# A five-layer network in fp32 pairs on one core: copies ahead of casts, a second raw chunk, and moved lows and splits

## The chip, the cores and the metric

The kernel runs on one core of one Trainium2 chip. The metric is the device time of the whole launch in microseconds (us), the median of several runs. The engines are TensorE (PE), VectorE (DVE), ScalarE (ACT), GpSimd (POOL) and SyncE (SP), which here issues most transfers.

## What is computed

x has 256 tokens and 1024 features. Four layers and a fifth one follow each other; cut to what matters:

```python
for layer in range(4):
    h = rmsnorm(x, attn_norm[layer])
    m = (diff_attention, stick_breaking_attention, sliding_window_attention)[layer % 3](h, ...)
    x = x + m @ w_o[layer]
    h = rmsnorm(x, ffn_norm[layer])
    x = x + (silu(conv(h @ w_gate)) * conv(h @ w_val)) @ w_down[layer]     # 2752 wide, 3 taps
x = rmsnorm(x, final_norm)
h = rms_norm(x, g_mix_pre)                                                 # the fifth layer
u, q, k, v = split(h @ w_in)
y = concatenate([pool_mixer(u), moba_attention(q, k, v)]) @ w_out          # pooled and attention halves
x = x + rms_norm(y, g_mix_post)
h = rms_norm(x, g_ffn_pre)
x = x + rms_norm((gelu(conv(h @ w_gate)) * (h @ w_val)) @ w_down, g_ffn_post)
x = x + (p @ w_ple) * sigmoid(x @ w_ple_gate)
```

Layers 0 and 3 use differential attention, layer 1 stick-breaking, layer 2 the sliding window. All is fp32.

## The kernel before

**Number pairs.** Every fp32 matrix is split in a high part (a cast to fp32r) and a low part (what is left). A product is three matmuls (high x high, high x low, low x high; L1681 to L1683, with the moving part 256 tokens). A weight chunk is 128 x 2048 numbers, which is two tiles of 128 output features over 8 tiles of 128 inputs: 48 matmuls. SP loads chunk after chunk into three raw buffers; ACT casts each to w_hi (L394); DVE subtracts to w_lo (L919, `split_to`), which signals lo_ready; w_hi and w_lo have five slots. SP loads chunk c once DVE has made the low of chunk c - 3.

**Stages.** STAGES lists da, sb, sw or mix (the projections and the attention of a layer; "mix" is the fifth, with pooled features), wo, up (22 chunks), down (8), and at the end gate. Each engine has one program, written out by hand in the same order of stages, and waits on semaphores for the others. `ahead(c, lead)` and `split_to(c)` put casts or lows of coming weight chunks at chosen places between other work. Results of a chunk go to one of three PSUM banks (pj, and val_bank in the up stage); bank_free gives a bank back.

**Normalisation.** To begin a stage before the root mean square is known, the first chunks are multiplied with the raw x times its gain (`raw_high` L448 on ACT, `raw_low` on DVE or POOL); DVE scales the result by rstd (`scaled_first` L985, or L1444 in the up stage). `raw_chunks` says where the normalised h takes over: `normalise` makes hf on DVE (L965), `split_h` casts it on ACT (L444), and the lows are made by DVE for even tiles (L961) and by POOL for odd ones (`low_odd`, L1544). PE puts the matmul that sums the squares (`statistic`, L1842) between tiles of the first raw chunk, at the place that one line gives:

```python
elif raw not in (None, "x", "raw") and k == {"d": 2, "w": 4}.get(raw[0], 5):
```

h_hi is written anew only when PE has used the raw tile (raw_used).

**Up stage.** Per chunk DVE has four taps of the convolution on top of ACT's first term (L1454, L854), then a w_lo, then the product (L1471); POOL casts the product and makes its low (L1652, L1655). In the first two chunks (one in the fifth layer) the taps read scaled copies in u_sb, not the banks.

**Attention.** In the sliding layer eight steps j each have on PE: transposes of the probabilities, scores for step j + 2, some projection or output products, and the head matmuls (L1916, L1917), which want ACT's copies of the transposed probabilities (`copy_probT`, L472) and, since all steps share one bank, DVE's low of the last step's result (`mix_low`, L1072, behind ACT's `mix_high`, L478). DVE reads the scores (L1001, `take`), makes a w_lo, divides by the sum (L1033 to L1040) and makes that low. In the stick-breaking layer POOL masks the probabilities (L1626) before the heads.

**Fifth layer.** `add_normed` (L1058, L1067) adds the normalised result of wo and of the last down stage to x; tmp holds a copy that ACT made of the PSUM bank (L785, L881).

## Time and profile before

| what | value |
|---|---|
| median of 3 runs | 1498.96 us (1498.57 to 1501.03) |
| profiled execution | 1498.88 us, its span 1497.2 us |
| PE busy | 1487.0 us, 99% of the span |
| DVE, ACT, POOL busy | 1063.5 (71%), 879.2 (59%), 336.2 us (22%) |
| matmuls | 11576 |
| transfers | 265.16 MB, mean 177 GB/s |

The span runs from the first to the last instruction of the program; the time of an execution also has what lies around it. Stages of the profile that the text speaks of: the first layer begins at 0, its up stage at some 124 us; the stick-breaking layer's attention ends at some 418, the sliding layer's attention runs from 614 to 694; the fifth layer begins at 1178.8, its up stage at 1263, its last down stage ends at 1464. A busy matmul row also counts the time in which it overlaps the next one, so starts tell more than durations; idle time stands in brackets behind a row, with the instruction whose semaphore ended it.

### The profile page before, as it was taken

The numbers are of one execution on the slowest core, as the hardware profiler recorded it, in microseconds if no ns is written. First come the engines' busy times: TensorE is split into PE (matmuls) and PEld (weight loads), VectorE is DVE, ScalarE is ACT, GpSimd is POOL, SyncE is SP. The second block draws the span as 40 slices with busy tenths as digits, with TensorE's granted clock in tenths as the row PEclk, the third lists the DMA queues.
The fourth block names the chain that finished last, engine by engine and source line by source line (L and its number), as shares of the span: only waits on it lengthen the run. The fifth ranks groups of instructions, "written<-read, shape, count | busy, mean of one in ns | idle before, by whom it ended". The sixth has DMA issues, their size and how long they took to land.

```text
span 1497.2 us, 28533 instructions
## 1 busy us (share of the span) xinstructions
PE 1487.0 (99%) x11576; PEld 1423.4 (95%) x11576; DVE 1063.5 (71%) x1734; ACT 879.2 (59%) x1405; POOL 336.2 (22%) x482
## 2 busy tenths in 40 slices
PE   9999999999999999999999999999999999999998
PEld 8999999899999998989999899999998899999998
DVE  7778877565578775786887566688775778776545
ACT  7777655456766554575656347766563567544343
POOL 2103222211142222213222221032222371221101
PEclk9999999999999999999999999999999999999999
DMA  7643656443336554552665545446554554365450
GB/s 272 204 162 124 242 184 218 169 163 147 117 138 218 205 190 177 187 180 85 216 207 183 188 170 178 155 145 221 197 192 177 173 191 169 114 228 194 164 209 29
DMA packets 39694, 265.16 MB, mean 177 GB/s; under 512 B 5247, under 2 KB 5562, under 8 KB 8976
## 3 DMA queue, kind: packets, MB, share of 16 engines
q1 hardware_dynamic: 36432, 255.54, 48.4%
q0 software_dynamic: 2992, 7.79, 2.3%
q8 instruction: 91, 1.49, 0.4%
q14 instruction: 35, 0.29, 0.1%
q10 hardware_dynamic: 144, 0.05, 0.0%
HBM read 262.24 MB, written 1.12 MB: 176 GB/s over the span
## 4 chain that ended last, share of the span: by engine, by line
PE 87%; DVE 8%; ACT 3%; issue 1%; POOL 0%; ACTq 0%
PE bank L1681 21%; PE bank L1682 20%; PE bank L1683 20%; PE bank L1692 9%; PE bank L1691 4%; PE bank L1733 4%; DVE w_lo L919 4%; PE bank L1742 2%; ACT w_hi L394 1%; PE bank L1916 1%; DVE tmp L1454 1%; PE bank L1897 1%; PE bank L1896 1%; DVE tmp L965 1%; PE bank L1905 1%
## 5 line engine op out<-in xcount | busy, mean ns | idle before, releaser
L919 DVE TENSOR_TENSOR w_lo<-w_raw,w_hi 128x2048 fp32r<-128x2048 f32 x239 | 553.0, 2321 | 72.5 <-ACT w_hi L394 72.3
L1681 PE MATMUL bank<-h_hi,w_hi 128*128 128x256 f32 x1968 | 561.2, 285 | 0.8 <-DVE w_lo L919 0.8
L1682 PE MATMUL bank<-h_lo,w_hi 128*128 128x256 f32 x1968 | 556.8, 283 | 0.0
L1683 PE MATMUL bank<-h_hi,w_lo 128*128 128x256 f32 x1968 | 556.8, 283 | 0.0
L394 ACT CAST w_hi<-w_raw 128x2048 fp32r<-128x2048 f32 x239 | 453.0, 1905 | 85.3 <-DMA w_raw<-w_std 64.4
L1681 PEld LDWEIGHTS bank<-h_hi,w_hi 128*128 128x128 f32 x1968 | 377.3, 192 | 6.4 <-issue 4.2
L1682 PEld LDWEIGHTS bank<-h_lo,w_hi 128*128 128x128 f32 x1968 | 377.4, 192 | 0.1
L1683 PEld LDWEIGHTS bank<-h_hi,w_lo 128*128 128x128 f32 x1968 | 377.3, 192 | 0.0
L1692 PE MATMUL bank<-act_both,w_hi 128*128 128x512 f32 x672 | 239.0, 399 | 0.0
L1454 DVE SCALAR_TENSOR_TENSOR tmp<-bank,par,tmp 128x255 f32<-128x255 f32 (+1 forms) x346 | 149.1, 476 | 94.6 <-ACT tmp L854 93.5
L1691 PE MATMUL bank<-act_both,w_lo 128*128 128x256 f32 x672 | 188.9, 281 | 0.0
L854 ACT ACTIVATE tmp<-bank,par 128x256 f32<-128x256 f32 x173 | 88.8, 558 | 157.0 <-PE bank L1683 156.9
L1692 PEld LDWEIGHTS bank<-act_both,w_hi 128*128 128x128 f32 x672 | 126.4, 188 | 30.0
L1652 POOL CAST act_both<-tmp 128x256 f32 x110 | 53.7, 488 | 440.2 <-DVE tmp L1471 336.5
L1681 PE MATMUL bank<-act_both,w_hi 128*128 128x256 f32 x516 | 149.2, 289 | 0.0
L1682 PE MATMUL bank<-act_both,w_hi 128*128 128x256 f32 x516 | 145.9, 283 | 0.0
L1683 PE MATMUL bank<-act_both,w_lo 128*128 128x256 f32 x516 | 145.9, 283 | 0.0
L1691 PEld LDWEIGHTS bank<-act_both,w_lo 128*128 128x128 f32 x672 | 127.0, 189 | 0.0
L1733 PE MATMUL bank<-h_hi,w_hi 128*128 128x256 f32 x384 | 102.5, 289 | 0.0
L1681 PEld LDWEIGHTS bank<-act_both,w_hi 128*128 128x128 f32 x516 | 98.7, 191 | 3.0 <-issue 2.7
L1733 PE MATMUL bank<-h_hi,w_lo 128*128 128x256 f32 x384 | 100.3, 283 | 0.0
L1682 PEld LDWEIGHTS bank<-act_both,w_hi 128*128 128x128 f32 x516 | 98.8, 191 | 0.1
(219 smaller groups left out, 2116.2 us busy)
## 6 DMA issues: line engine op xcount, KB each, us to landing
w_raw<-w_std SPq DMA_DIRECT2D x239, 1024.0 KB, 4.8
act_both<-vec_dram POOLq DMA_DIRECT2D x56, 128.0 KB, 3.4
w_raw<-w_std SPq DMA_DIRECT2D x3, 512.0 KB, 7.8
x<-xT SPq DMA_DIRECT2D x2, 512.0 KB, 5.2
out<-x SPq DMA_DIRECT2D x3, 256.0 KB, 2.0
w_raw<-w_std SPq DMA_DIRECT2D x2, 256.0 KB, 4.8
par<-params SPq DMA_DIRECT2D x1, 446.0 KB, 6.0
cst<-consts SPq DMA_DIRECT2D x1, 256.0 KB, 8.8
```

Source lines behind the costliest of these rows:

```text
L394: act.copy(w_hi[:, n % SLOTS, :], w_raw[:, n % RAW, :]).then_inc(hi_ready, 1)
L854: act.activation(to[:, slot, :], source, ACT.Identity, bias=col(3), scale=col(2)).then_inc(conv_init, 1)
L919: dve.tensor_tensor(w_lo[:, n % SLOTS, :], w_raw[:, n % RAW, :], w_hi[:, n % SLOTS, :].bitcast(F32), ALU.subtract).then_inc(lo_ready, 1)
L1454: return dve.scalar_tensor_tensor(to[:, slot, lag:S], source(v)[:, 0:S - lag], par[:, bass.ds(at + (4 * v + 2 - lag), 1)], to[:, slot, lag:S],
L1652: pool.tensor_copy(act_hi[:, bass.ds(j, 1), :].squeeze(1) if not isinstance(j, int) else act_hi[rows, j, :], cval[rows, slot, :]).then_inc ...
L1681: pe.matmul(dst, wh, xh, start=first, stop=False, skip_group_check=shared)
L1682: pe.matmul(dst, wh, xl, start=False, stop=False, skip_group_check=shared)
L1683: done = pe.matmul(dst, wl, xh, start=False, stop=last, skip_group_check=shared)
L1691: pe.matmul(bank[:, 0:S], wl, xh, start=start and k == 0, stop=False, skip_group_check=True)
L1692: done = pe.matmul(bank[:, :], wh, pair, start=False, stop=stop and k == len(weights) - 1, skip_group_check=True)
L1733: pe.matmul(dst, a, b, start=k == 0 and w is wh and (n == 0 or not shared), stop=False, skip_group_check=shared)
L1742: done = pe.matmul(dst, a, b, start=False, stop=k == DT - 1, skip_group_check=shared)
```

## The change

1. **Sliding layer.** On ACT the copies of the probabilities for steps 2 and 6 go ahead of a weight cast or of the exponentials, `mix_high` ahead of `evac_q`, and in step 5 ahead of the copies of step 6 and of the exponentials. On DVE `mix_low` goes ahead of `divide`.
2. **Stick-breaking layer, last group.** DVE's first `mix_low` goes between the two w_lo.
3. **First layer.** ACT's cast and DVE's low of weight chunk 2 go ahead of the rstd.
4. **Up stages of layers 0 to 3.** In the second chunk, as in the first, DVE's w_lo goes ahead of the taps; PE's fifth chunk waits for the scaled tiles of the second and no longer for its bank.
5. **Fifth layer, start.** The second chunk is multiplied with the raw x too; DVE scales its result, which ACT copied before; the statistic is asked for behind tile 5 instead of tile 2.
6. **Last up stage.** DVE makes all eight lows of h, each one tile behind the normalised tile (`every=True`); POOL's `low_odd` is left out there.
7. **Gains.** ACT multiplies by mix_post and ffn_post when it copies the banks to tmp (two instructions of 256 for one of 512 in wo), and `add_normed` on DVE is a product of two tensors instead of three factors.

```diff
@@ -292,3 +292,3 @@
 
-            return 3 if app == 0 else 2 if app % 2 and app < 9 else 1
+            return 3 if app == 0 else 2 if app % 2 and app < 9 or app == 8 else 1
 
...
@@ -567,2 +567,4 @@
                     groups = 2 if kind == "mix" else 4
+                    if c0 == 0:
+                        split_to(2)
                     (both_rms if prev == "down3" else rms)(SUMS[prev][2])
...
@@ -581,8 +583,4 @@
                         for k in range(2):
-                            if k:
-                                act.wait_ge(bank_free, RING + c0 + 1)
-                                act.wait_ge(used, c0 + k + 1)
-                                act.copy(u_sb[:, 2 * k:2 * k + 2, :].rearrange("p a b -> p (a b)"),
-                                         pj[slot_of(c0, k)][:, :]).then_inc(bank_free, 1)
                             ahead(c0 + k)
+                        act.wait_ge(bank_free, RING + c0 + 2)
                         lead = 2
...
@@ -745,10 +743,16 @@
                             q, s = half + j, s_half + j
-                            copy_probT(s, j % 2, 2)
+                            if j not in (2, 6):
+                                copy_probT(s, j % 2, 2)
                             if j == 5:
                                 ahead(c0 + 6, HIGH)
+                                mix_high(q, j)
+                                copy_probT(s + 1, 0, 2)
                             if j < 6:
                                 exps(s + 2, j % 2, j + 3)
+                            if j != 5:
+                                mix_high(q, j)
                             if j in (1, 3):
                                 evac_q(c0 + 4 + j // 2, j // 2)
-                            mix_high(q, j)
+                            if j == 1:
+                                copy_probT(s + 1, 0, 2)
                             if j < 3:
...
@@ -784,3 +788,4 @@
                                     mixed_gains[:, t:t + 1]).then_inc(mixed_high, 1)
-                        done = act.copy(tmp[:, a:b, :].rearrange("p a b -> p (a b)"), source)
+                        for t in range(a, b):
+                            done = act.mul(tmp[:, t, :], source[:, (t - a) * S:(t - a + 1) * S], param("mix_post", t))
                         if k != 3:
...
@@ -880,3 +885,4 @@
                             squares(name, k, pj[slot_of(c0, k)][:, 0:S])
-                            act.copy(tmp[:, k, :], pj[slot_of(c0, k)][:, 0:S]).then_inc(bank_free, 1)
+                            act.mul(tmp[:, k, :], pj[slot_of(c0, k)][:, 0:S], param("ffn_post", k))\
+                               .then_inc(bank_free, 1)
                             if k == 2:
...
@@ -954,3 +960,3 @@
 
-            def normalise(app, norm, behind=None):
+            def normalise(app, norm, behind=None, every=False):
 
...
@@ -961,3 +967,3 @@
                     dve.tensor_tensor(h_lo[:, k, :], hf[:, k, :], h_hi[:, k, :].bitcast(F32),
-                                      ALU.subtract).then_inc(h_lo_even, 1)
+                                      ALU.subtract).then_inc(h_lo_odd if k % 2 else h_lo_even, 1)
 
...
@@ -966,4 +972,10 @@
                                              ALU.mult, ALU.mult).then_inc(hf_done, 1)
-                    if k % 2 and k > 1 and behind is None:
+                    if every:
+                        if k:
+                            low(k - 1)
+                    elif k % 2 and k > 1 and behind is None:
                         low(k - 3)
+                if every:
+                    low(DT - 1)
+                    return
                 if behind is not None:
...
@@ -1054,7 +1066,6 @@
 
-            def add_normed(gain, factor, signal, after):
+            def add_normed(factor, signal, after):
 
                 def scaled(k):
-                    dve.scalar_tensor_tensor(tmp[:, k, :], tmp[:, k, :], param(gain, k),
-                                             factor, ALU.mult, ALU.mult).then_inc(dve_step, 1)
+                    dve.tensor_tensor(tmp[:, k, :], tmp[:, k, :], factor, ALU.mult).then_inc(dve_step, 1)
                     steps[0] += 1
...
@@ -1141,5 +1152,5 @@
 
+                split_to(2)
                 dve.wait_ge(rstd_done, 1)
                 scaled(0, 1, 2, 3)
-                split_to(2)
                 scaled_first(0, proj, (0.125, 1.0))
...
@@ -1202,2 +1213,4 @@
                                      {"mix": (1.0, 1.0), "sw": (0.125, 0.125)}.get(kind, (0.125, 1.0)))
+                        if kind == "mix":
+                            scaled_first(c0 + 1, u_sb[:, 2:4, :], (1.0, 1.0))
                     app += 1
...
@@ -1312,4 +1325,5 @@
                                 ahead(c0 + n)
-                                ahead(c0 + n, HIGH)
                             mix_low(q, i * 2)
+                            if not more:
+                                ahead(c0 + n, HIGH)
                             mix_low(q + 1, i * 2 + 1)
...
@@ -1339,5 +1353,5 @@
                                 ahead(c0 + 3 + min(j, 4))
+                            mix_low(half + j, j)
                             if j < 6:
                                 steps[0] += divide(s_half + j + 2, j % 2, True, steps[0])
-                            mix_low(half + j, j)
                         half += 8
...
@@ -1395,5 +1409,5 @@
                         dve.wait_ge(rstd_done, SUMS[name][2] + 1)
-                        add_normed("mix_post", mix_rstd, x_ready, sum_behind)
+                        add_normed(mix_rstd, x_ready, sum_behind)
                         ahead(c0 + 2, AHEAD)
-                        normalise(app, SUMS["res_a"][2])
+                        normalise(app, SUMS["res_a"][2], every=True)
                         ahead(c0 + 1, AHEAD)
...
@@ -1445,4 +1459,3 @@
                                                       ALU.mult).then_inc(first_scaled, 1)
-                                if j == 0:
-                                    split_to(weights_of(layer, c) + RING)
+                                split_to(weights_of(layer, c) + RING)
 
...
@@ -1639,3 +1652,4 @@
                     raw_low(app)
-                    low_odd(app, hf)
+                    if layer < 4:
+                        low_odd(app, hf)
                     app += 1
...
@@ -1750,3 +1764,3 @@
                             statistic("x")
-                    elif raw not in (None, "x", "raw") and k == {"d": 2, "w": 4}.get(raw[0], 5):
+                    elif raw not in (None, "x", "raw") and k == (5 if raw == "down3" else {"d": 2, "w": 4}.get(raw[0], 5)):
                         statistic(raw)
...
@@ -1768,6 +1782,6 @@
 
-            def project(c, slot, app=None, raw=None):
+            def project(c, slot, app=None, raw=None, release=True):
 
                 if app is not None:
-                    pair(c, (pj[slot][:, 0:S], pj[slot][:, S:2 * S]), app, raw=raw)
+                    pair(c, (pj[slot][:, 0:S], pj[slot][:, S:2 * S]), app, raw=raw, release=release)
                     return
...
@@ -1949,5 +1963,6 @@
                     g0 = c0 + lead
-                    for k in range(lead):
-                        project(c0 + k, slot_of(c0, k), app, prev if k == 0 else None)
-                    project(g0, slot_of(g0, 0), app if lead == 0 else None, prev if lead == 0 else None)
+                    if lead:
+                        project(c0, slot_of(c0, 0), app, prev, False)
+                        project(c0 + 1, slot_of(c0, 1), app, "raw")
+                    project(g0, slot_of(g0, 0), app, None if lead else prev)
                     project(g0 + 1, slot_of(g0, 1), app if lead == 0 else None, "second" if c0 == 0 else None)
...
@@ -2218,5 +2233,5 @@
                     def up(c, k):
-                        if k == RING and layer < 4:
+                        if k in (RING, RING + 1) and layer < 4:
                             pe.wait_ge(lo_ready, weights_of(layer, c) + 1)
-                            pe.wait_ge(first_scaled, first_scaled_count(ffn, 1))
+                            pe.wait_ge(first_scaled, first_scaled_count(ffn, 2 * (k - RING) + 1))
                         else:
```

The two hunks that are left out take the gain's argument away from one more call and replace mixed_gains by ffn_pre in `low_of_mixed`.

How the order moves, at three places. First DVE in the up stage of layer 0, first and second chunk (u_sb: scaled copies, tmp: the convolution's sums). Before:

```order
L1444 TENSOR_TENSOR u_sb<-bank,rstd 128x256 [waits used]
L1444 TENSOR_TENSOR u_sb<-bank,rstd 128x256
L919 TENSOR_TENSOR w_lo<-w_raw,w_hi 128x2048 [waits hi_ready]
L1454 SCALAR_TENSOR_TENSOR tmp<-u_sb,par,tmp 128x255 [waits conv_init] x2
L1454 SCALAR_TENSOR_TENSOR tmp<-u_sb,par,tmp 128x254 [waits conv_part] x2
L1471 TENSOR_TENSOR tmp<-tmp 128x256 [waits bank_free,gated]
L1444 TENSOR_TENSOR u_sb<-bank,rstd 128x256 [waits used]
L1444 TENSOR_TENSOR u_sb<-bank,rstd 128x256
L1454 SCALAR_TENSOR_TENSOR tmp<-u_sb,par,tmp 128x255 [waits conv_init] x2
L1454 SCALAR_TENSOR_TENSOR tmp<-u_sb,par,tmp 128x254 [waits conv_part] x2
L919 TENSOR_TENSOR w_lo<-w_raw,w_hi 128x2048 [waits hi_ready]
L1471 TENSOR_TENSOR tmp<-tmp 128x256 [waits bank_free,gated]
```

And now:

```order
L1458 TENSOR_TENSOR u_sb<-bank,rstd 128x256 [waits used]
L1458 TENSOR_TENSOR u_sb<-bank,rstd 128x256
L925 TENSOR_TENSOR w_lo<-w_raw,w_hi 128x2048 [waits hi_ready]
L1467 SCALAR_TENSOR_TENSOR tmp<-u_sb,par,tmp 128x255 [waits conv_init] x2
L1467 SCALAR_TENSOR_TENSOR tmp<-u_sb,par,tmp 128x254 [waits conv_part] x2
L1484 TENSOR_TENSOR tmp<-tmp 128x256 [waits bank_free,gated]
L1458 TENSOR_TENSOR u_sb<-bank,rstd 128x256 [waits used]
L1458 TENSOR_TENSOR u_sb<-bank,rstd 128x256
L925 TENSOR_TENSOR w_lo<-w_raw,w_hi 128x2048 [waits hi_ready]
L1467 SCALAR_TENSOR_TENSOR tmp<-u_sb,par,tmp 128x255 [waits conv_init] x2
L1467 SCALAR_TENSOR_TENSOR tmp<-u_sb,par,tmp 128x254 [waits conv_part] x2
L1484 TENSOR_TENSOR tmp<-tmp 128x256 [waits bank_free,gated]
```

The w_lo of the second chunk now stands ahead of its four taps.

Second, DVE at the last up stage, where it normalises the eight tiles (tmp: hf). Before:

```order
L965 SCALAR_TENSOR_TENSOR tmp<-x,par,rstd 128x256 [waits rstd_done]
L965 SCALAR_TENSOR_TENSOR tmp<-x,par,rstd 128x256 x3
L961 TENSOR_TENSOR h_lo<-tmp,h_hi 128x256 [waits h_hi_done]
L965 SCALAR_TENSOR_TENSOR tmp<-x,par,rstd 128x256 x2
L961 TENSOR_TENSOR h_lo<-tmp,h_hi 128x256 [waits h_hi_done]
L965 SCALAR_TENSOR_TENSOR tmp<-x,par,rstd 128x256 x2
L961 TENSOR_TENSOR h_lo<-tmp,h_hi 128x256 [waits h_hi_done] x2
```

And now, the first tiles of eight:

```order
L971 SCALAR_TENSOR_TENSOR tmp<-x,par,rstd 128x256 [waits rstd_done]
L971 SCALAR_TENSOR_TENSOR tmp<-x,par,rstd 128x256
L967 TENSOR_TENSOR h_lo<-tmp,h_hi 128x256 [waits h_hi_done]
L971 SCALAR_TENSOR_TENSOR tmp<-x,par,rstd 128x256
L967 TENSOR_TENSOR h_lo<-tmp,h_hi 128x256 [waits h_hi_done]
L971 SCALAR_TENSOR_TENSOR tmp<-x,par,rstd 128x256
L967 TENSOR_TENSOR h_lo<-tmp,h_hi 128x256 [waits h_hi_done]
L971 SCALAR_TENSOR_TENSOR tmp<-x,par,rstd 128x256
L967 TENSOR_TENSOR h_lo<-tmp,h_hi 128x256 [waits h_hi_done]
L971 SCALAR_TENSOR_TENSOR tmp<-x,par,rstd 128x256
L967 TENSOR_TENSOR h_lo<-tmp,h_hi 128x256 [waits h_hi_done]
```

Each normalised tile but the first is now followed by the low of the one before; before, four of eight lows were made here, behind pairs.

Third, ACT in the sliding layer, from the end of step 1's exponentials to the start of step 2's (proj: evacuated queries, act_both: the mixed tile's high, tmp from the bank: probabilities). Before:

```order
L464 ACTIVATE tmp,small<-tmp,small 128x256
L730 ACTIVATE proj<-bank 128x512 [waits used]
L478 CAST act_both<-bank 128x256 [waits pv_done]
L394 CAST w_hi<-w_raw 128x2048 [waits arrived1,used]
L472 COPY tmp<-bank 128x384 [waits trans_done]
L472 COPY tmp<-bank 128x384
L460 ACTIVATE small<-small 128x4 [waits sink_shift,nmax_ready]
```

And now:

```order
L464 ACTIVATE tmp,small<-tmp,small 128x256
L478 CAST act_both<-bank 128x256 [waits pv_done]
L728 ACTIVATE proj<-bank 128x512 [waits used]
L472 COPY tmp<-bank 128x384 [waits trans_done]
L472 COPY tmp<-bank 128x384
L394 CAST w_hi<-w_raw 128x2048 [waits arrived1,used]
L460 ACTIVATE small<-small 128x4 [waits sink_shift,nmax_ready]
```

The mixed tile's high now goes ahead of the queries, and the two copies ahead of the cast of a weight chunk.

## Rows read from the trace of the kernel before

**Rows 1.** The page, busy time, share of the span and instructions by engine

```profile
PE 1487.0 (99%) x11576; PEld 1423.4 (95%) x11576; DVE 1063.5 (71%) x1734; ACT 879.2 (59%) x1405; POOL 336.2 (22%) x482
```

**Rows 2.** List of waits of PE, whole span: waiter <- releaser: us in total, times, longest

```profile
PE bank L1842 <- DVE acc L953: 1.1, 1, 1.1
PE bank L1681 <- DVE w_lo L919: 1.0, 5, 0.2
PE bank L1916 <- DVE act_both L1072: 0.9, 2, 0.5
PE bank L1742 <- DVE h_lo L961: 0.7, 2, 0.4
...
PE bank L1742 <- POOL h_lo L1544: 0.5, 1, 0.5
PE bank L1916 <- ACT tmp L472: 0.5, 3, 0.2
```

**Rows 3.** Timeline of PE, first layer: start us, us, engine line op [idle before <-releaser]

```profile
23.32 0.40 PE L1742 MATMUL bank<-h_lo,w_hi 128*128 128x256 f32 x2
23.91 0.39 PE L1681 MATMUL bank<-w_hi,h_hi 128*128 128x256 f32 x1 [0.18 <-DVE w_lo L919]
24.13 0.28 PE L1682 MATMUL bank<-w_lo,h_hi 128*128 128x256 f32 x1
```

**Rows 4.** Timelines of DVE, ACT, POOL, PE, first layer's up stage

```profile
137.85 2.86 DVE L919 TENSOR_TENSOR w_lo<-w_raw,w_hi 128x2048 fp32r<-128x2048 f32 x1
...
138.72 1.89 ACT L394 CAST w_hi<-w_raw 128x2048 fp32r<-128x2048 f32 x1
...
143.23 0.75 DVE L1444 TENSOR_TENSOR u_sb<-bank,rstd 128x256 f32<-128x256 f32 x2
144.40 1.89 DVE L1454 SCALAR_TENSOR_TENSOR tmp<-u_sb,par,tmp 128x255 f32<-128x255 f32 x4 [0.42 <-ACT tmp L854]
...
144.08 0.74 POOL L1655 TENSOR_TENSOR act_both<-tmp,act_both 128x256 f32 x1 [0.19 <-POOL act_both L1652]
...
146.21 2.28 DVE L919 TENSOR_TENSOR w_lo<-w_raw,w_hi 128x2048 fp32r<-128x2048 f32 x1
...
148.55 0.39 PE L1681 MATMUL bank<-h_hi,w_hi 128*128 128x256 f32 x1 [0.22 <-DVE w_lo L919]
```

**Rows 5.** Timelines and POOL's line L1626 (ns min/median/max), stick-breaking layer, last group

```profile
408.28 4.48 DVE L919 TENSOR_TENSOR w_lo<-w_raw,w_hi 128x2048 fp32r<-128x2048 f32 x2
...
410.95 3.15 POOL L1626 TENSOR_SCALAR_AFFINE_SELECT tmp<-tmp 128x256 f32<-128x256 f32 x4 [3.94 <-ACT tmp L691]
...
L1626 POOL TENSOR_SCALAR_AFFINE_SELECT tmp<-tmp x32: 401/406/2075, 335.6 to 413.7; 128x256 f32<-128x256 f32 x32
...
413.49 0.66 PE L1916 MATMUL bank<-tmp,vtok 128*64 128x256 f32 x4 [0.53 <-issue]
```

**Rows 6.** Timelines of ACT and DVE, sliding layer

```profile
650.99 1.91 ACT L394 CAST w_hi<-w_raw 128x2048 fp32r<-128x2048 f32 x1
652.80 0.85 ACT L472 COPY tmp<-bank 128x384 f32<-128x384 f32 x2
...
675.02 0.42 DVE L1072 TENSOR_TENSOR act_both<-bank,act_both 128x256 fp32r<-128x256 f32 x1
```

**Rows 7.** Timeline of DVE, start of the pooled layer

```profile
1182.07 0.48 DVE L978 SCALAR_TENSOR_TENSOR h_lo<-x,both_gains,h_hi 128x256 fp32r<-128x256 f32 x1
```

**Rows 8.** Timeline of DVE, last up stage

```profile
1276.18 1.67 DVE L965 SCALAR_TENSOR_TENSOR tmp<-x,par,rstd 128x256 f32<-128x256 f32 x4 [1.85 <-ACT rstd L426]
...
1278.11 1.84 DVE L965 SCALAR_TENSOR_TENSOR tmp<-x,par,rstd 128x256 f32<-128x256 f32 x2
```

**Rows 9.** Timelines of DVE and POOL, end of the last down stage

```profile
1471.51 0.47 DVE L1058 SCALAR_TENSOR_TENSOR tmp<-tmp,par,rstd 128x256 f32<-128x256 f32 x1
...
1472.84 2.36 POOL L1544 TENSOR_TENSOR h_lo<-x,h_hi 128x256 fp32r<-128x256 f32 x2 [1.53 <-ACT h_hi L893]
```

**Rows 10.** List of waits of all engines, whole span

```profile
ACT w_hi L394 <- DMA w_raw<-w_std: 64.4, 32, 5.7
```

More of the change, by code:

```diff
@@ L1180, in low_of_mixed @@
                 dve.wait_ge(bank_free, RING + c + k // 2 + 1)
-                dve.scalar_tensor_tensor(mixed_lo[:, k, :], tmp[:, k, :], mixed_gains[:, k:k + 1],
+                dve.scalar_tensor_tensor(mixed_lo[:, k, :], tmp[:, k, :], param("ffn_pre", k),
                                          mixed_hi[:, k, :].bitcast(F32), ALU.mult, ALU.subtract)\
@@ L1312, in group @@
                                 ahead(c0 + n)
+                            mix_low(q, i * 2)
+                            if not more:
                                 ahead(c0 + n, HIGH)
-                            mix_low(q, i * 2)
                             mix_low(q + 1, i * 2 + 1)
@@ L1510, in low @@
                                                   ALU.subtract).then_inc(h_lo_even, 1)
-                        add_normed("ffn_post", rstd[:, :], hf_done, low)
+                        add_normed(rstd[:, :], hf_done, low)
                         split_to(CHUNKS)
```

## The prediction

> **What bounds the kernel.** I read the page first: PE is busy for 99% of the span at the full granted clock [rows 1]. So the time can only fall where PE stands still, and the list of who PE waited for comes next [rows 2]. In those six rows and one more wait of 0.53 in the stick-breaking layer, PE idles only 5.2 us in 1497. The largest is one wait of 1.1 for DVE's sum of squares, then five of together 1.0 for DVE's low half of a weight chunk (w_lo), two of 0.9 for DVE's low of a mixed tile (act_both L1072), two of 0.7 for DVE's low of h, one of 0.5 for POOL's low of h, and three of 0.5 for ACT's copy of probabilities. This change goes at nearly all of them, so the sum is a sum of small waits.
>
> **What one wait costs.** Idle time understates it. In the first layer a matmul of 256 columns starts every 0.12 us [rows 3] (a pair lasts 0.40, one 0.28). After the pair at 23.32 the next was due at 23.56. It came at 23.91, 0.35 late, with 0.18 of idle; then its own successor came 0.22 behind it, not 0.12. So a wait costs its idle plus 0.17 for the restart and 0.10 for the next weight load: idle + 0.27. Ahead of a statistic or of the small head matmuls I count only idle + 0.17, since those restart in any case.
>
> **The change part by part** (all against the profiled execution, 1498.88 us, a span of 1497.2 and 1.7 around it; it stands 0.1 below the median of 1498.96).
>
> First layer: ACT casts chunk 2 ahead of the rstd, and DVE makes its low ahead of the four normalised tiles. The wait that was just read was for this low: **0.45** (0.18 + 0.27). What pays is those tiles, later by up to 0.8; no wait of PE hangs on them [rows 2].
>
> Up stages of the first four layers: the timelines show the second step [rows 4]. DVE scales two tiles (143.23), runs four taps (144.40), then makes w_lo (146.21 to 148.49), and PE starts the chunk at 148.55 with 0.22 idle. Now w_lo goes ahead of the taps: it starts at about 143.97 and ends at 146.25, 1.9 before PE was due (148.16), and PE asks the bank of that step only for the scaled tiles. Four of the five waits go: 0.82 + 4 x 0.27 = **1.90**. What is later: taps (1.89) end at 148.15, the activation and the product (0.4 each) at 149.0, the next taps (some 1.7) at 150.7, the next w_lo (2.28) at 153.0. PE wants that at 148.16 + 48 x 0.12 = 153.9, so it is covered by 0.9. What uses that cover up is in the first rival.
>
> Stick-breaking layer, last group: DVE's second w_lo runs from about 410.5 to 412.76, and POOL's first mask of that place takes 2.08 where the median mask takes 0.41 [rows 5]. PE's head matmuls need the first two masks. The change puts DVE's low of the mixed tile, which waits for those very heads, between the two w_lo, so the second cannot run beside the masks: they would end at 411.8, and PE was due at 412.8. Gain 0.53 + 0.17, less what the switch of matmul kind costs anyway: **0.67**. The second w_lo ends near 417.5; it is the next up stage's first chunk, some 10 us early.
>
> Sliding layer: a cast of 1.91 stands in front of the two copies (652.80) [rows 6] for which PE waited 0.2, one of ACT's three [rows 2], and DVE's low of a mixed tile came only at 675.02 to 675.44, behind the division; that is the longer of its two waits [rows 2], 0.5. Copies now go ahead of the cast and lows ahead of the divisions. But DVE now waits for ACT's high of the tile, some 0.15 to 0.25 in four steps, and the late DVE makes the next exponentials and so the next copies late. The bounds are a loss of 0.5 and the whole 1.6 (0.9 + 0.2 idle and 3 x 0.17). Walking both engines through the eight steps, I find the copy of the fifth step only 0.2 and the low of the seventh 0.4 earlier, and take **0.4**.
>
> Pooled layer: the sum of squares is asked for behind the sixth tile instead of the third, 3 x 6 x 0.12 = 2.2 later, while DVE is 1.1 late. The wait goes: 1.07 + 0.17 = **1.25**. The last low of the raw tiles is there at 1182.55 [rows 7], before PE reaches the last tile at 1184.8. The second chunk is raw too, so the normalised h is needed one chunk (5.76) later; but ACT can write its last tile only when that chunk ends. Behind it come that cast (0.4), the cast of the weights (1.91 [rows 6]) and their low (2.28 [rows 4]), together 4.6, for a chunk due 5.76 later. Covered by 1.1. Two more scalings on DVE, 0.75, run while ACT casts.
>
> Last up stage: DVE makes all lows of h, one behind each normalised tile. Four tiles took 1.67, then two took 1.84, POOL's lows running beside them [rows 8]. With 0.42 for a tile and 0.37 for its low, the first low is there at 1277.5 instead of 1278.19, and each next 0.79 later; PE eats a tile in 0.72 and first asks at 1277.8. All eight hold, the last by little: both waits go, 0.7 + 2 x 0.27 = **1.24**. The scaled gains moved to ACT are off every path.
>
> Last down stage: ACT now multiplies by the gain, so DVE's eight products take 0.41 rather than 0.47 [rows 9], and seven of them stand ahead of the tile whose low POOL makes from 1472.84. That is 0.4 to 0.5 earlier against a wait of 0.5 + 0.27. Bounds 0 and 0.77, taken **0.6**.
>
> The sum is 0.45 + 1.90 + 0.67 + 0.40 + 1.25 + 1.24 + 0.60 = 6.5 us, and with it 1492.4. Nothing is added to PE.
>
> A rule speaks against the up stages. The row: a w_lo beside POOL's lows of h took 2.86 instead of 2.28 (137.85 [rows 4]), and POOL's low of the product, due at 144.08, now falls on the moved w_lo. The Trainium skill (SBUF — State Buffer, "SBUF: two separate sides") says that a VectorE instruction with two SBUF inputs and a GpSimd one exclude each other for a whole instruction, and the loser stands fully still. By that rule POOL's 0.7 would be pushed behind w_lo and then hold the taps; the sum would be 3.8 instead of 6.5 where both collisions happen in all four layers. That result is the first rival, priced from rows.
>
> **The rivals.** (1) *The saved wait comes back one chunk later.* If the moved w_lo takes 2.86 and POOL's 0.74 [rows 4] then stands ahead of the taps, the chain above is 1.3 longer and the w_lo of the next chunk ends at 154.3: idle 0.4 + 0.27, four times 2.7. With nothing from the sliding layer the gain is 6.5 - 2.7 - 0.4 = 3.4: **1495.5**. For it: the two engines stretch each other in two places [rows 4, 5]. Against: one collision alone (0.58 or 0.74) stays inside 0.9.
>
> (2) *The waits only change their names.* In the sliding layer, the last up and the last down stage three engines are within some tenths of each other; if those give nothing (2.24), one of the two collisions' waits is left in each up (0.3 x 4) and the stick-breaking masks stay late (0.67), 2.4 is left: **1496.5**, no change that can be told.
>
> (3) *Slower.* In the up stages the w_lo ahead of the taps waits for ACT's cast of the same chunk, and the taps, the banks and the next low wait behind it. The cast ended at 140.6 (138.72 + 1.89 [rows 4]), 3.3 before DVE comes. ACT waited for a weight transfer 32 times, at most 5.7 [rows 10]. Here it waited none. Should the moved low start later than 143.97 by more than 0.9, PE waits the rest; the kernel is slower by 3 us, 0.2%, from 1.9 of waiting in each layer on (4 x 1.9 = 4.6 + 3), so from a cast that is 3.3 + 0.9 + 1.9 = 6.1 late. At 7 late the up stages lose 4 x 2.8 = 11.2 and the rest gains 4.6: **1505.5**. Only an unusual state of the queues would do it.
>
> That the change does not do what it says is hardly a rival: the order of instructions shows each move.
>
> **How the numbers follow.** Forecast 0.67, rival (1) 0.19, rival (2) 0.09, rival (3) 0.05. The likeliest is **1492.4 us**; its own range is 1491.0 (sliding 1.6, last down 0.77) to 1493.9 (sliding -0.5, last down 0.2). The range of 8 in 10 takes in rival (1): 1491.0 to 1495.8. A measurement of this kernel can tell about 0.2%, 3 us, from no change. The forecast and rival (1) are faster by more: 0.86; rival (2) the same: 0.09; rival (3) slower: 0.05.
>
> **What would show it.** In the profile of after, PE's list of waits should have no w_lo, no acc and no h_lo of DVE, and the "issue" wait before the heads of the stick-breaking layer should be gone, its first mask at 0.41. The four up stages should start their fifth chunk 5.76 behind the fourth. What should be left is a few tenths for act_both or for ACT's copies in the sliding layer. Rival (1) shows as PE waiting for w_lo at the sixth chunk of an up stage, rival (3) as DVE waiting for w_hi there. A wait of PE over 0.5 in the pooled layer's fourth chunk would prove my cover of 1.1 wrong.

## The result, and the profile after

The changed kernel takes 1501.44 us (median of 20 runs, 1500.58 to 1504.35); the kernel before, on the same chip, 1498.89 (20 runs). The ratio is 1.0016, with a 95% interval of 1.0009 to 1.0022: **2.5 us slower, where 6.5 faster was forecast.** The profiled execution took 1500.86, a span of 1499.2 (before 1497.2).

The page's busy times (the first line below, to be held against [rows 1]) show POOL 11 us busier with fewer instructions. Then comes the list of waits of PE, whole span, which answers to [rows 2]:

```profile
PE 1487.4 (99%) x11576; PEld 1424.8 (95%) x11576; DVE 1063.4 (71%) x1740; ACT 880.6 (59%) x1407; POOL 347.6 (23%) x478
```

```profile
PE bank L1910 <- DVE small L1013: 2.1, 1, 2.1
PE bank L1756 <- POOL h_lo L1557: 1.9, 1, 1.9
PE bank L1695 <- ACT vtok L512: 1.5, 1, 1.5
...
PE bank L1910 <- ACT proj L728: 0.6, 1, 0.6
PE bank L1930 <- ACT tmp L472: 0.3, 2, 0.2
PE bank L1930 <- DVE act_both L1083: 0.2, 1, 0.2
```

("small" is the row maxima that DVE makes when it takes the scores, "vtok" ACT's copy of a value tile. A wait of 1.4 for the rstd at the very start stands in both kernels.) Every wait that the forecast wanted gone is gone: w_lo, acc, DVE's h_lo, the masks. Three long ones are new. To see when the time was won and lost, the matmuls of both traces are matched one by one: how far does the new kernel's start lie ahead of the old one's, read where the lead has settled behind each place?

| place | forecast | read in the traces |
|---|---|---|
| warm-up before the first layer | 0 | 0.4 ahead (TensorE reached its full clock sooner in this execution) |
| first layer, chunk 2 | 0.45 | 0.43 won |
| four up stages | 1.90 | 0.48 + 0.44 + 0.43 + 0.44 = 1.79 won |
| stick-breaking | 0.67 | 0.61 won |
| sliding | 0.40 | 0.55 won, behind a new wait of 0.56 |
| pooled layer, its start | 1.25 | 1.4 won |
| pooled layer, 1228 to 1237 | 0 | **5.3 lost** |
| wo of the pooled layer, where ACT now multiplies by the gain | 0 | 0.15 lost |
| last up | 1.24 | 1.1 won (1.4, less 0.3 at a short new wait at 1289.3) |
| last down | 0.60 | **2.8 lost** |

So 5.9 was won where the forecast had 5.9 (its sum without the last down stage), and 8.3 was lost, nearly all of it in two places. With the 0.4 of the warm-up this makes the 2.0 by which the span grew.

**The pooled layer.** The timeline of the changed kernel, DVE, POOL and PE, where it waits:

```profile
1225.09 2.21 POOL L1552 DMA_DIRECT2D act_both<-vec_dram  x4 [0.30 <-POOL act_both L1622]
...
1228.75 0.28 PE L1697 MATMUL bank<-act_both,w_lo 128*128 128x256 f32 x1
1229.78 0.06 DVE L1006 MEMSET wait_mark<- 128x1 f32 x1 [6.87 <-DMA act_both<-vec_dram]
...
1231.17 0.50 PE L1910 MATMUL bank<-proj 64*128 64x128 f32 x4 [2.14 <-DVE small L1013]
...
1233.64 0.58 PE L1695 MATMUL bank<-act_both,w_hi 128*128 128x256 f32 x1 [1.54 <-ACT vtok L512]
1234.02 0.42 PE L1696 MATMUL bank<-act_both,w_hi 128*128 128x256 f32 x1
1234.24 0.41 PE L1697 MATMUL bank<-act_both,w_lo 128*128 128x256 f32 x1
```

PE waits for DVE to take the scores. DVE stood idle 6.87 for the bias tables, which are added to the scores, and their four loads were issued by POOL only at 1225.09, because they stand behind POOL's pooling. Before, POOL issued them at 1224.04, PE came to this place 5.2 later than it does now, and DVE did not wait for a table. Why POOL is late is read in its own timeline, first group of the pooling, changed kernel (the last line is DVE's):

```profile
1189.15 0.19 POOL L1613 COPY sq<-u_sb 128x1 f32<-128x1 f32 x1 [0.31 <-DVE u_sb L997]
1189.29 0.61 POOL L1614 TENSOR_TENSOR sq<-u_sb 128x255 f32<-128x255 f32 x1
1189.98 2.25 POOL L1617 TENSOR_TENSOR sq<-sq,par 128x16 f32<-128x16 f32 x1
1192.21 2.84 POOL L1618 TENSOR_SCALAR sq<-sq 128x240 f32<-128x240 f32 x1
...
1189.86 4.51 DVE L925 TENSOR_TENSOR w_lo<-w_raw,w_hi 128x2048 fp32r<-128x2048 f32 x2 [0.78 <-ACT w_hi L394]
```

and the same two instructions before:

```profile
1195.00 0.22 POOL L1604 TENSOR_TENSOR sq<-sq,par 128x16 f32<-128x16 f32 x1
1195.19 0.81 POOL L1605 TENSOR_SCALAR sq<-sq 128x240 f32<-128x240 f32 x1
```

Sixteen columns take 2.25 instead of 0.22: POOL stands still while DVE makes a w_lo, and DVE's two w_lo are hardly stretched (4.51 for both, 2.28 for one alone). Before, the two w_lo had a pause of 0.97 between them (1192.02 and 1195.28); now ACT casts both chunks in one go, the two w_lo follow each other, and both lie on POOL. Of POOL's 40 pooling instructions 7 take over 2 us (before 4), and the 40 together 34.3 instead of 28.9. This is the rule that the prediction weighed for the up stages (the Trainium skill, SBUF — State Buffer, "SBUF: two separate sides": the one that starts first has the shared ports for its whole instruction). The trace agrees: the w_lo began at 1189.86, POOL's sixteen columns at 1189.98, and POOL waited. Here, unlike in the up stages, POOL has to be on time.

**TensorE's clock.** The last rows of PE above take 0.42 and 0.41, not 0.28. Stretches of the changed kernel: length, busy time of PE, PEld, DVE, ACT and POOL with their instructions, then the granted clock, the DMA share and GB/s:

```profile
1229.00:1234.00 5.00, 1.32 (x10) 0.92 (x10) 4.15 (x14) 2.74 (x11) 0.00 (x0) 0.96 0.05 14
1234.00:1237.00 3.00, 3.00 (x15) 3.00 (x15) 2.97 (x17) 1.55 (x5) 0.00 (x0) 0.50 0.86 279
1237.00:1240.00 3.00, 3.00 (x26) 2.57 (x26) 1.57 (x7) 3.00 (x12) 0.00 (x0) 1.00 0.17 71
...
1472.00:1476.00 4.00, 4.00 (x21) 4.00 (x22) 2.59 (x2) 3.98 (x3) 2.21 (x3) 0.57 0.00 0
```

0.50 is 1.2 of 2.4 GHz: 15 matmuls in 3 us instead of 26. In all, PE lost 5.3 at the first place, of which 3.7 are the two waits themselves; the other 1.7 are the low clock and the restarts. At the last down stage it lost 2.8, of which 1.4 are the longer wait (1.86 instead of 0.50) and 1.5 the low clock.

**The last down stage.** Its result is added to x tile by tile on DVE, ACT casts each tile, and DVE and POOL make the lows for the matmuls that follow (even tiles DVE, odd ones POOL). DVE and POOL, changed kernel:

```profile
1467.25 0.42 DVE L1078 TENSOR_TENSOR x<-x,tmp 128x256 f32<-128x256 f32 x1
1467.59 0.42 DVE L1070 TENSOR_TENSOR tmp<-tmp,rstd 128x256 f32<-128x256 f32 x1
1467.92 0.42 DVE L1078 TENSOR_TENSOR x<-x,tmp 128x256 f32<-128x256 f32 x1
...
1470.60 0.75 DVE L1078 TENSOR_TENSOR x<-x,tmp 128x256 f32<-128x256 f32 x2
1471.49 0.73 DVE L1521 TENSOR_TENSOR h_lo<-x,h_hi 128x256 fp32r<-128x256 f32 x1
...
1467.19 4.75 POOL L1557 TENSOR_TENSOR h_lo<-x,h_hi 128x256 fp32r<-128x256 f32 x1 [60.25 <-ACT h_hi L899]
1471.90 2.31 POOL L1557 TENSOR_TENSOR h_lo<-x,h_hi 128x256 fp32r<-128x256 f32 x3
```

and before:

```profile
1468.35 0.41 DVE L1067 TENSOR_TENSOR x<-x,tmp 128x256 f32<-128x256 f32 x1
1468.68 0.96 DVE L1058 SCALAR_TENSOR_TENSOR tmp<-tmp,par,rstd 128x256 f32<-128x256 f32 x1
...
1470.63 0.95 DVE L1067 TENSOR_TENSOR x<-x,tmp 128x256 f32<-128x256 f32 x1
...
1468.22 1.14 POOL L1544 TENSOR_TENSOR h_lo<-x,h_hi 128x256 fp32r<-128x256 f32 x1 [60.43 <-ACT h_hi L893]
1470.50 0.81 POOL L1544 TENSOR_TENSOR h_lo<-x,h_hi 128x256 fp32r<-128x256 f32 x1 [1.14 <-ACT h_hi L893]
1472.84 2.36 POOL L1544 TENSOR_TENSOR h_lo<-x,h_hi 128x256 fp32r<-128x256 f32 x2 [1.53 <-ACT h_hi L893]
```

POOL's four lows were busy for 4.3 before and are for 7.0 now, and the difference lies in the first one: 4.75 instead of 1.14. It begins at 1467.19, twelve DVE instructions pass, each with its 0.42 and start behind start by 0.33 to 0.34, and only when DVE pauses, at 1471.35, does POOL get through; the other three take 2.31 together. PE waits for this very first low, from 1470.13 to 1471.99. Before, two DVE instructions were stretched to 0.96 and 0.95 while POOL had its turn, so the first two lows came in time, and PE waited 0.50 for the third. Whether it is the kind of the DVE instruction is the first question below.

### The profile page after: what moved, and what is told of

Read it like the earlier page. It is cut to its first block, busy times and chain, and to the rows that moved or that the text cites. A ratio compares the mean times of both kernels' runs of the same rounds, so it can differ in the third digit from the quotient of the medians.

```text
span 1499.2 us, 28537 instructions
## 1 busy us (share of the span) xinstructions
PE 1487.4 (99%) x11576; PEld 1424.8 (95%) x11576; DVE 1063.4 (71%) x1740; ACT 880.6 (59%) x1407; POOL 347.6 (23%) x478
## 4 chain that ended last, share of the span: by engine, by line
PE 94%; POOL 3%; DVE 1%; ACT 1%; DMA 1%; issue 0%; ACTq 0%; DVEq 0%; POOLq 0%
PE bank L1695 21%; PE bank L1696 21%; PE bank L1697 21%; PE bank L1706 11%; PE bank L1747 6%; PE bank L1705 5%; PE bank L1756 3%; PE bank L1930 1%; PE bank L1911 1%; PE bank L1910 1%; PE bank L1919 1%; PE bank L2279 1%; POOL sq L1618 0%; POOL sq L1617 0%; ACT tmp L464 0%
```

## The experiments

Times are medians. The kernel before took 1498.91, 1499.14 and 1498.95 in the three sets of runs; the changed kernel was not run again in them, so a difference to it across sets can be off by some tenths. "Won" and "lost at a place" are read as in the table, from the profiled execution.

**stt_product.** One line in `add_normed`:

```diff
-                    dve.tensor_tensor(tmp[:, k, :], tmp[:, k, :], factor, ALU.mult).then_inc(dve_step, 1)
+                    dve.scalar_tensor_tensor(tmp[:, k, :], tmp[:, k, :], 1.0, factor,
+                                             ALU.mult, ALU.mult).then_inc(dve_step, 1)
```

> The changed kernel, but add_normed on DVE multiplies with three factors again (tmp x 1.0 x rstd): only the kind of the instruction is undone, the gains stay with ACT. Theory A (a product of two tensors on DVE shuts POOL out while it runs, one of three factors does not): POOL's four lows of the last down stage take some 1.1 each as before the change, not 1.78; PE's wait of 1.9 for h_lo goes or falls under 0.3, and the matmuls that follow keep starting every 0.12 us instead of 0.21; together 3.2 to 3.6 us less than the changed kernel. Rival (POOL is slow there because DVE and ACT follow more densely, whatever the instruction): POOL's lows stay over 1.5 and the time changes by less than 0.5.

Measured: 1501.35. POOL's lows still take 7.0 together (the first 4.75), and the wait is 1.9. Theory A in this form fell, and so far the rival stands. But the product took 0.42, while the old one, with a gain per partition, takes 0.48; so the instruction was not yet the old one.

**bias_early.** In POOL's pooling loop:

```diff
                         for g, w in enumerate(WINDOWS):
+                            if g == 3:
+                                for h in range(2, halves):
+                                    bias_dma(table, s_half + h, h % 2, h)
```

with the later place left out.

> The changed kernel, but POOL issues the bias loads of heads 2 and 3 of the fifth layer ahead of the fourth pooling group, not behind it. Theory B (PE's scores waited for DVE, DVE for the bias, and the bias for POOL's pooling, which DVE's w_lo had stretched): the waits of 2.1 and 1.5 at 1229 to 1234 go, and with them the slow matmuls up to 1237, 5.2 to 5.6 us less than the changed kernel, though POOL's pooling takes as long as in it. Rival (DVE's own lows, or ACT's copies behind the exponentials, are what is late): a wait over 0.5 of scores or of vtok stays, and the gain is under 2.

Measured: 1496.78, 4.7 less than the changed kernel. The waits for the scores and for vtok are gone, and the clock stays full; theory B holds. At this place 3.6 is won back and not 5.2 to 5.6, since the next wait appears. The rest of the difference is not the edit's: in this execution the clock did not fall in the last down stage either, although the wait of 1.86 there is unchanged (1.5), and a wait in the first layer, of which more below, took 0.65. The new wait names what is late now:

```profile
PE bank L1759 <- POOL h_lo L1557: 1.9, 1, 1.9
PE bank L1698 <- POOL act_both L1625: 1.5, 1, 1.5
```

PE needs POOL's last pooled low 1.5 before it is there: the loads, now ahead of it, take 2.2 of POOL's time, and that low itself took 2.72 beside a w_lo.

The low clock behind the wait of 1.86 is also not the same in every execution of a kernel. Of the ten of this one, five show a mean granted clock of 1.0 and took 1495.66 to 1496.69, five show 0.998 or 0.999 and took 1496.88 to 1497.16; the profiled one is of the first kind. All twenty of the changed kernel show 0.997 or 0.998.

**both_mended.** The two edits together.

> Both edits on the changed kernel. The two places lie 240 us apart, so the gains should add: 8.4 to 9.2 us less than the changed kernel, which is 1492.3 to 1493.0, the value that was forecast. Rival (the gains of the other places are smaller than the forecast's sum, or one mended place makes a new wait): 1494 or more.

Measured: 1496.88, the same as bias_early, since the first edit does nothing. Missed; its rival, 1494 or more, came.

**gains_alone.** The kernel before, with the hunks of the gains.

> The kernel before with the move of the gains alone (ACT multiplies by mix_post and ffn_post, DVE's product has two factors). Theory A: POOL's lows take 1.7 to 1.8, the wait for POOL's h_lo grows from 0.5 to some 1.9 and matmuls behind it start every 0.21 us for some 3.5 us: 2.4 to 2.9 us slower than before. The forecast had 0.6 faster.

Measured: 1501.57, 2.7 slower (ratio 1.0017, 1.0008 to 1.0026), POOL's lows 7.0, the wait 1.9, and 16 slow matmuls behind it. This part alone costs the 2.7, whatever its mechanism. Seven of its ten executions show a mean clock of 1.0, three (the profiled one among them) 0.999. The median of the seven is 1500.53, 1.6 over the kernel before: the wait that is 1.4 longer and the 0.15 in wo.

**ones_column.** The scalar comes from memory again:

```diff
+                    dve.scalar_tensor_tensor(tmp[:, k, :], tmp[:, k, :], ones[:, k:k + 1], factor,
+                                             ALU.mult, ALU.mult).then_inc(dve_step, 1)
```

> The changed kernel with a three-factor product in add_normed whose scalar is read from a column of ones, one number per partition, as the gain was before the change; the gains stay with ACT. The product with the constant 1.0 in the instruction had changed nothing and took 0.42, not 0.48. Theory A2 (POOL gets in between two DVE instructions only where the next one has a per-partition scalar to fetch first): the product takes 0.47, POOL's four lows of the last down stage 1.0 to 1.2 each, PE's wait there falls from 1.9 to under 0.5 and the matmuls behind it start every 0.12 us: 2.7 to 3.5 us less than the changed kernel. Rival (it is ACT's multiplication, or the stage's earlier start, that makes POOL slow): no change over 0.4.

Measured: 1499.21, 2.2 less than the changed kernel and level with the kernel before (ratio 1.0003, 0.9991 to 1.0015). That is under the expected 2.7 to 3.5. At the place itself all 2.8 come back; in the pooled layer this execution lost 5.9 and not 5.3. POOL in the last down stage:

```profile
1467.69 1.14 POOL L1558 TENSOR_TENSOR h_lo<-x,h_hi 128x256 fp32r<-128x256 f32 x1 [60.43 <-ACT h_hi L899]
1469.96 0.81 POOL L1558 TENSOR_TENSOR h_lo<-x,h_hi 128x256 fp32r<-128x256 f32 x1 [1.14 <-ACT h_hi L899]
1472.31 2.35 POOL L1558 TENSOR_TENSOR h_lo<-x,h_hi 128x256 fp32r<-128x256 f32 x2 [1.54 <-ACT h_hi L899]
```

Row for row the old pattern, the wait is 0.5 and the clock full there, with ACT still multiplying the gains. Against stt_product only the place of the scalar differs, so the rival of this run (ACT's multiplication, or the stage's earlier start) is out. What is shown is that with this operand POOL's first low takes 1.14 and without it 4.75. That POOL slips in *while the scalar is fetched* is not shown, and the rows speak against it in this narrow form: of the two DVE instructions that stretch, the second (1470.63 before) is the sum x + tmp, which has no such scalar. The product with the scalar from memory also takes 0.06 longer, and the next instruction starts 0.40 behind it and not 0.33; a denser order as the cause, the rival of stt_product, was not separated from the operand.

**gains_bias.** Gains back on DVE, bias loads early.

> The changed kernel with the gains back on DVE as before the change, and the bias loads of heads 2 and 3 ahead of the fourth pooling group. Theory A2: against the kernel with the early bias alone, the wait of 1.9 for POOL's h_lo falls to 0.5: 1.3 to 1.6 less, 1495.2 to 1495.5. The wait of 1.5 for the pooled low stays. Rival (the late low of h comes from something else in the change): still 1.9 there.

Measured: 1494.48. The wait is 0.5 again. The gain over bias_early is 2.3, more than the expected 1.3 to 1.6. Against the five executions of bias_early with a clock of 1.0 (median 1496.27) it is 1.8, of which the wait is 1.4 and the place in wo 0.15; the rest fits the other five, with their lower clock, and its wait in the first layer. None of this was tried apart.

**gains_pooled_undone.** The changed kernel without its parts 5 and 7.

> The changed kernel without the move of the gains and without the second raw chunk and the later statistic of the fifth layer; the other five parts stay. If only these two parts lose, what is left is the gain read between the two traces at the other places: 0.25 to 0.45 in the first layer, 1.4 to 1.5 in the four up stages, 0.7 in the stick-breaking layer, 0.7 in the sliding layer, 0.9 to 1.2 in the last up stage, 4.0 to 4.6 in all: 1494.3 to 1494.9. Rival (the fifth layer is upset by whatever makes PE earlier): a new wait of over 1 there, 1496 or more.

Measured: 1493.76 (ratio 0.9959, 0.9946 to 0.9973), 0.5 below the expected range. The expected sum took the up stages at 1.4 to 1.5, where the settled lead shows 1.8, and the profiled execution is the slowest of the five and has a wait of 0.43 in the first layer; what is left is some tenths that no place explains. The other five parts are worth some 5 us, and no new wait comes up in the fifth layer. The rival is out.

**pooled_alone.** The kernel before with part 5 alone.

> The kernel before with the fifth layer's second raw chunk and later statistic alone. Theory B (this part starts POOL's pooling under two w_lo in a row and takes from PE's lead over the bias what PE gains at the start): 2.2 are gained at 1180, then PE waits some 2 for the scores' bias and 1.5 for vtok, with slow matmuls behind: 2.5 to 4 us slower than before. Rival (the lost cover comes from the earlier stages' gains): at most one wait under 1, and 1 to 2 us faster. The forecast had 1.25 faster.

Measured: 1503.48, 4.3 slower (1.0028, 1.0019 to 1.0038), a little beyond the expected; only 1.4 is won at the start of the layer, not 2.2, and 5.7 is lost behind it. Its two longest waits:

```profile
PE bank L1894 <- DVE small L997: 2.5, 1, 2.5
PE bank L1679 <- ACT vtok L512: 1.5, 1, 1.5
```

So the part brings its loss along; the earlier stages' gains did not use up the cover.

**best_sp.** Gains back on DVE, and SP issues the bias loads, with semaphores of their own:

```diff
             for c in range(1, CHUNKS):
+                if c == CHUNKS - 41:
+                    for h in range(2, 4):
+                        sp.wait_ge(scores_taken, 24 + h - 1)
+                        for m, to in enumerate((act_hi, act_lo)):
...
+                            sp.dma_start(to[:, 8 + h % 2, :].bitcast(F32), src).then_inc(bias_sp[h % 2], 16)
```

> The changed kernel with the gains back on DVE, and the bias loads of heads 2 and 3 of the fifth layer issued by SP instead of POOL, ahead of the weight load that follows their heads' scores. In the kernel with the loads moved ahead on POOL, their four issues took 2.2 of POOL's time and PE then waited 1.5 for the last pooled low. Theory B: POOL's chain ends 2.2 sooner, that wait goes, and nothing new comes: 1.6 to 1.9 less than with both edits on POOL (1494.5), 1492.6 to 1492.9, with the 2.2 gained at the start of the fifth layer kept. Rival (the pooling is late for another reason, or SP's loads hold up the weights): a wait over 0.5 stays, 1493.8 or more.

Measured: **1492.72** (five runs, 1492.42 to 1493.77; ratio 0.9959, 0.9946 to 0.9973), inside the expected range and 8.7 below the changed kernel. The start of the layer gives 1.4 here too, not the 2.2 of the expectation. Its list of waits:

```profile
PE bank L1965 <- DVE rstd L1109: 1.4, 1, 1.4
PE bank L1920 <- ACT proj L736: 0.6, 1, 0.6
PE bank L1766 <- POOL h_lo L1567: 0.5, 1, 0.5
PE bank L1705 <- DVE tmp L1497: 0.3, 1, 0.3
PE bank L1940 <- ACT tmp L480: 0.3, 2, 0.2
PE bank L1940 <- DVE act_both L1093: 0.2, 1, 0.2
```

POOL's pooling is as long as in the changed kernel (the two instructions shown above again take 7.0 and 7.3 in their four groups), but nobody waits for it: this version keeps part 5's gain.

**pool_late_2 and pool_late_4.** POOL copies 512 numbers per partition two or four times ahead of the last low of h (work that only takes time), in gains_pooled_undone. The question is when the clock falls behind a wait.

> The kernel without the gains' move and without the fifth layer's second raw chunk (1493.8), with two copies of 512 numbers on POOL ahead of the last low of h in the last down stage, work that only takes time. It makes one wait of PE of some 0.8 to 1.6 there. If a wait costs its idle and 0.17 to 0.27 and no more, the time rises by just that. If TensorE's clock falls behind a wait of this size, the matmuls after it start every 0.21 us for a stretch and the time rises by some 1.5 more.

Measured: 1494.83, 1.1 more. In the profiled execution (1498.1, well above its median) two waits of together 0.8 stand at the place, and the clock stays full. Of itself it shows little about the clock; but that execution had a wait of 1.92 in the first layer, and the low clock behind it.

> The same with four such copies: one wait of 2.4 to 3.4 of PE. In the changed kernel a wait of 1.86 at this place was followed by matmuls at half speed for 3 us (some 1.4 us lost), in two other kernels the same wait was not. If the length of the wait decides, the low clock comes here for certain and costs at least 1.4 beyond the idle; if it does not come here either, the length alone does not decide.

Measured: 1502.19, 8.4 more; the wait was 5.5, larger than meant. Behind it, the same columns as above:

```profile
1477.00:1483.00 6.00, 0.50 (x5) 0.29 (x4) 4.92 (x2) 3.44 (x3) 5.90 (x4) 0.81 0.00 0
1483.00:1487.50 4.50, 4.50 (x21) 4.50 (x22) 1.39 (x2) 0.60 (x1) 0.00 (x0) 0.50 0.16 58
1487.50:1490.00 2.50, 2.50 (x23) 2.50 (x23) 0.00 (x0) 0.00 (x0) 0.00 (x0) 0.99 0.03 7
```

That is 5.5 more of idle (6.0 in two waits, instead of 0.5) and 2.1 from the low clock. All ten executions show a mean clock of 0.995 to 0.999. But the wait is so far above the 2.4 to 3.4 that were meant that it says nothing of waits just above 1.86.

**A wait in the first layer.** In several executions PE waited near 32 us for DVE's low of h, 0.4 to 0.6 in most of them, but 1.92 in the profiled one of pool_late_2 and 4.36 in that of pool_late_4. In the two large ones DVE's row names the cause (pool_late_4):

```profile
33.86 0.06 DVE L1008 MEMSET wait_mark<- 128x1 f32 x1 [4.38 <-DMA act_both<-vec_dram]
```

DVE stood idle 4.38 (in pool_late_2 1.94, in bias_early 0.65) for the bias tables. It is the same chain as in the pooled layer: POOL issued these loads at 25.61, 24.90 and 24.49, in the changed kernel at 23.45, since it waited for another transfer to land. The edits of these runs do not touch the first layer, and the time of issue differs with the old first layer too (22.89 in the kernel before, 24.34 in gains_alone, where PE waited 0.51). So it is a difference between executions; whether the change makes the wait likelier was not tried.

## Why the prediction was wrong, point by point

- **First layer, up stages, stick-breaking, sliding, last up, pooled start: right in mechanism and nearly so in size.** All those waits went. "A wait costs its idle + 0.27" held: the first layer gave 0.43 for 0.45, the up stages 1.79 for 1.90. The sliding layer gave 0.55 for 0.40, although the queries, now behind `mix_high`, came late and PE waited 0.56 for them until 661.44; the small sum came out of bounds from -0.5 to 1.6, so the agreement is in part luck. The forecast's sum of all these was 5.9, the traces show 5.9.
- **The collision of rival (1) came and cost nothing.** At 143.04 the moved w_lo met POOL's low of the product. The rival had w_lo stretched to 2.86 and POOL's 0.74 ahead of the taps. The loser was POOL, which started second, with 2.69 instead of 0.74; w_lo kept its 2.28, the taps took 2.15 instead of 1.89, and the next chunk was on time:

```profile
143.04 2.28 DVE L925 TENSOR_TENSOR w_lo<-w_raw,w_hi 128x2048 fp32r<-128x2048 f32 x1
...
143.23 2.69 POOL L1669 TENSOR_TENSOR act_both<-tmp,act_both 128x256 f32 x1 [0.19 <-POOL act_both L1666]
```

- **Pooled layer, the failed step:** the term has its gain of 1.25 and nothing against it ("Covered by 1.1", "Nothing is added to PE"). The cover of 1.1 itself held: it was counted along ACT and DVE through the second raw chunk, and no wait came in the fourth chunk. What was put at nothing without a reason is the path over POOL, though POOL's whole pooling starts at the very tiles that part 5 delivers, and the bias loads stand behind it. The runs show 5.3 lost there, 5.7 with part 5 alone, and none once SP issues the loads. Two rows of the trace of before would have shown it: the loads were issued at 1224.04, and DVE took those scores at 1230.56. With the 4.7 from issue to use that the changed trace shows, the slack was 1.8. The change made PE 1.4 earlier there and POOL 4.9 later, both against the start of the layer (5.4 of stretching, less 0.5 of earlier start): 6.3 against 1.8, and DVE came 4.5 after the scores were there. The sign that the prediction gave, a wait in the fourth chunk, looked in the wrong place; the wait came some 35 us later.
- **Last down stage, the failed step:** "DVE's eight products take 0.41 rather than 0.47 ... That is 0.4 to 0.5 earlier." DVE was indeed earlier. But the trace of before has POOL's low in a turn with DVE's stretched product, and the new instruction was priced by its length alone, not by what it leaves for POOL. POOL's first low took 4.75 instead of 1.14, and 2.8 was lost where 0.6 was to be won. The bound "0" on this term was no bound: a loss was excluded without a reason.
- **The price of a long wait** has a third part that the forecast lacked. The two places cost 1.7 and 1.5 beyond their idle, nearly all of it at 1.2 GHz: some 3 of the 8.3 that were lost.
- **Two slips in the working, without weight for the outcome.** The largest wait of before is not the 1.1 but 1.4 for the rstd at the very start, which the change leaves alone. And the upper end of the forecast's own range, with the sliding layer at -0.5 and the last down stage at 0.2, comes to 1493.7, not 1493.9.
- **The other rivals.** Rival (3), slower through a late cast in the up stages, did not occur; the kernel got slower by a mechanism that no rival named. Rival (2) did not occur either.

## What to carry to other kernels

When a change makes the bound engine earlier, or moves the start of a side chain, walk every engine's chain from the place that moves to its last consumer and note the slack at its end, the lightly loaded engine's too: POOL was 22% busy and decided this case. Where DVE and POOL both work against a deadline, ask of each DVE instruction whether it lets POOL in; a shorter form of it can be the dearer one. And move small loads that only wait in a busy engine's queue to a queue that has time.

## What the runs showed of the hardware that I had not expected

- A stream of DVE instructions with two tensors in SBUF, one behind the other every 0.33 to 0.34, held a POOL instruction off across twelve of them: it took 4.75, until DVE paused. With every second or third of them reading a scalar per partition (0.48 instead of 0.42) the same one took 1.14. The same three-factor form with its constant in the instruction did not help (4.75).
- A POOL instruction that starts just behind a w_lo stands until the w_lo ends and then takes its own time: 2.25 for 16 columns instead of 0.22. One with a single tensor (TENSOR_SCALAR, 2.84 instead of 0.81) is hit as well.
- TensorE fell to 1.2 GHz for 3 to 5 us of its work behind single waits of 1.86 (three kernels), 1.92, 4.36 and 5.5, and behind the pairs of 2.14 to 2.49 and 0.81 to 1.54. It did not behind waits up to 1.5, nor behind the same wait of 1.86 at the same place in the profiled executions of two other kernels (bias_early and both_mended). The mean clocks of their other executions differ from one to the next, so it looks like a matter of the execution and not of the kernel. The length alone does not decide at 1.86; what else does stays open.
